# Four gate tiles of the mixer moved ahead of the index logits and ahead of the sparse branch's logits

## The reference, cut to what matters

```python
proj = h @ w_in                                  # fox qkv, dsa qkv, index q/k/w, sb qkv, gates
o_fox = fox_attention(fq, fk, fv, log_f)         # 6 heads: softmax attention with forget terms
o_dsa = dsa_sparse_attention(dq, dk, dv, q_idx, k_idx, w_idx, 64)
                                                 # 5 heads; a score from 8 index heads picks 64 keys per query
o_sb  = stick_breaking_attention(sq, sk, sv)     # 5 heads
g = sigmoid(gates.reshape(b, s, 3, 1024))
merged = g[:, :, 0] * (o_fox @ w_fox_out) + g[:, :, 1] * (o_dsa @ w_dsa_out) + g[:, :, 2] * (o_sb @ w_sb_out)
x = x + merged @ w_out
```

## Time and profile before

| what | value |
|---|---|
| median of 3 executions | 2512.96 us (2512.77 to 2521.8) |
| the profiled execution | 2521.01 us |
| its span, first to last instruction | 2519.2 us |
| mean granted TensorE clock | 0.986 |
| TensorE busy | 2451.9 us (97%) |
| VectorE busy | 827.4 us (33%) |
| ScalarE busy | 248.1 us (10%) |
| DMA | 340.40 MB, 135 GB/s |

### The profile page before, as it was taken

The page is one execution under the profiler, slowest core; times in us unless marked ns, Lnnn a source line. Parts: engine busy times, 40 slices in busy tenths (PEclk is TensorE's granted clock), DMA queues, the critical chain, the costliest instruction groups (busy, mean ns, idle before and its releaser), DMA issues.

```text
span 2519.2 us, 28186 instructions
## 1 busy us (share of the span) xinstructions
PE 2451.9 (97%) x11907; PEld 2111.4 (84%) x11907; DVE 827.4 (33%) x1734; ACT 248.1 (10%) x424; POOL 14.1 (1%) x27
## 2 busy tenths in 40 slices
PE   6999999999999999999999999998999999999998
PEld 5888888878888888888877888887878888878887
DVE  2111323734210111022273331105646512566531
ACT  1000003201100000000311110001210000120000
POOL 0000000000000000000000000000000000000000
PEclk9999999999999999999999999999899999899999
DMA  6544543334554555454523445545335545435542
GB/s 187 155 140 155 130 139 101 101 117 134 140 155 156 150 151 151 150 146 104 153 76 117 134 134 153 155 143 126 110 98 153 143 153 135 110 117 150 156 146 80
DMA packets 491781, 340.40 MB, mean 135 GB/s; under 512 B 47836, under 2 KB 468488, under 8 KB 491656
## 3 DMA queue, kind: packets, MB, share of 16 engines
q1 hardware_dynamic: 487056, 335.53, 46.4%
q10 hardware_dynamic: 4328, 2.02, 0.3%
q0 software_dynamic: 272, 1.05, 0.1%
HBM read 337.52 MB, written 1.05 MB: 134 GB/s over the span
## 4 chain that ended last, share of the span: by engine, by line
PE 82%; issue 10%; DVE 5%; ACTq 1%; DVEq 1%; ACT 0%; DMA 0%; POOLq 0%; POOL 0%
PE bank L494 48%; PE bank L536 21%; PE bank L500 4%; PE bank L768 2%; ACTq L1033 1%; PE bank L894 1%; PE bank L771 1%; DVE work L1245 1%; PE bank L623 1%; PE bank L716 0%; PE bank L714 0%; DVE topw L1569 0%; DVE arena L1248 0%; DVE small L1587 0%; DVEq L1590 0%
## 5 line engine op out<-in xcount | busy, mean ns | idle before, releaser
L494 PE MATMUL bank<-hT,ring 128*128 128x256 f32 (+1 forms) x5952 | 1308.0, 381 | 11.8 <-DVE work L1245 7.7
L494 PEld LDWEIGHTS bank<-hT,ring 128*128 128x128 f32 (+1 forms) x5952 | 1124.2, 189 | 183.3 <-issue 11.2
L536 PE MATMUL bank<-work,ring 128*128 128x256 f32 (+1 forms) x2368 | 515.6, 380 | 0.0
L536 PEld LDWEIGHTS bank<-work,ring 128*128 128x128 f32 (+1 forms) x2368 | 448.4, 190 | 66.4 <-issue 6.1
L1248 DVE SCALAR_TENSOR_TENSOR xT<-bank,xT 128x512 f32<-128x512 f32 x48 | 33.2, 692 | 490.4 <-PE bank L536 490.4
L1245 DVE TENSOR_TENSOR a<-e,bank 128x256 f32<-128x256 f32 x80 | 33.7, 421 | 472.7 <-PE bank L494 472.7
L494 PE MATMUL bank<-xg,ring 128*128 128x256 f32 x640 | 148.9, 390 | 5.7 <-DMA ring<-in_ffn_w_gu 3.6
L494 PEld LDWEIGHTS bank<-xg,ring 128*128 128x128 f32 x640 | 123.1, 195 | 23.4 <-DMA ring<-in_ffn_w_gu 4.0
L1039 ACT ACTIVATE hT<-xT 128x512 f32<-128x512 f32 x56 | 35.4, 632 | 689.3 <-DVE xT L1248 672.9
L536 PE MATMUL bank<-arena,ring 128*128 128x256 f32 x384 | 88.5, 391 | 4.6 <-DVE arena L1248 4.6
L536 PEld LDWEIGHTS bank<-arena,ring 128*128 128x128 f32 x384 | 74.7, 196 | 15.8 <-DVE arena L1248 5.0
(11 more groups left out here) (249 smaller groups left out, 1349.5 us busy)
## 6 DMA issues: line engine op xcount, KB each, us to landing
ring<-in_ffn_w_gu SPq DMA_DIRECT2D x176, 512.0 KB, 5.1
ring<-in_ffn_w_down SPq DMA_DIRECT2D x64, 1024.0 KB, 4.8
ring<-in_ffn_w_up SPq DMA_DIRECT2D x84, 512.0 KB, 5.3
ring<-in_w_in SPq DMA_DIRECT2D x78, 512.0 KB, 5.1
ring<-in_w_in SPq DMA_DIRECT2D x26, 1024.0 KB, 5.2
ring<-in_w_out SPq DMA_DIRECT2D x16, 1024.0 KB, 4.8
ring<-in_ca_w_kv SPq DMA_DIRECT2D x8, 1024.0 KB, 5.1
ring<-in_w_in SPq DMA_DIRECT2D x24, 256.0 KB, 4.0
```

Of the source, the lines that this page charges most:

```text
L494: mm = pe.matmul(b[0:width, 0:S], view[:, c, a:a + width], src[:, c, :], start=(c == 0), stop=(c == C - 1))
L536: return pe.matmul(acc(m), view[0:r, k % 2, m * P:(m + 1) * P], self.src[0:r, self.order[k], :], start=(k == 0 and m % 2 == 0), stop=(k == ...
```

## The change

In `attention1` of TensorE's program, the gate tiles G10 and G11 are computed ahead of the index logits instead of behind them, and G18 and G19 ahead of the sparse logits instead of behind them. No other engine's program changes, the number of instructions is the same, and so is the order in which gate tiles, loads and semaphore counts follow each other among themselves.

```diff
                         mm.then_inc(sem["attn_done"], 1)
+                gate_tiles(2)
                 for t in range(T):
                     w = P * (t + 1)
                     for g in sharing(N_IDX):
...
-                gate_tiles(8)
+                gate_tiles(6)
                 pe.wait_ge(sem["operand_ready"], n("operand_ready"))
                 turn(sc, N_FOX)
...
                     mm.then_inc(sem["attn_done"], 1)
+                gate_tiles(2)
                 for t in range(T):
                     w = P * (t + 1)
                     for g in sharing(N_DSA):
...
-                gate_tiles(6)
+                gate_tiles(4)
                 pe.wait_ge(sem["operand_ready"], n("operand_ready"))
                 turn(sc, N_DSA)
```

## The result

The changed kernel is slower by 0.37%: the ratio to the kernel before is 1.0037 (1.0025 to 1.0049), +9.3 us (+6.3 to +12.3). The median of 12 executions is 2526.19 us against 2513.82 us of 12 before. The medians lie 12.4 us apart, just outside the ratio's interval. The executions of both kernels come in two groups 6 to 7 us apart (before: eight at 2512.5 to 2514.8, four at 2519.0 to 2521.8; after: four at 2520.5 to 2521.6, eight at 2525.8 to 2528.8), and each median lies in the larger group, the lower one before and the upper one after. The forecast was +5.1 us and 2518.1 us; the direction and the mechanism held, the size was too small, and the median lies 0.2 us above the top of the range.

What follows compares the result with a forecast made beforehand. TensorE, busy 97% of the span, was taken as the bound, with VectorE's 39.3 us block setting its second wait. +6.7 us at equal clocks less 1.6 of clock gave +5.1: 2512.96 + 5.1 = 2518.1 us, range 2512 to 2526.

Steps and rivals of the forecast that it cites:

- What bounds the stage: Between forget logits and second transposes: VectorE's fixed 39.3 us block, first index bank to copy of first weighted sum.
- Part 1: G10, G11 ahead of index logits: VectorE starts 6.57 us later; waits of 1.6 us before G12, 1.2 before G16.
- Part 2: G18, G19 ahead of sparse logits: TensorE idle 4.5 us instead of 1.54; shorter work behind it gives back 3.2 us.
- The sum at equal clocks: Both mixers: 6.57 - 3.2 = +3.4 us for a layer, +6.7 us for both, if the sparse softmax stays hidden.
- The clock term: Loss to TensorE's slow clock behind the waits, both layers: 3.8 us after against 5.4 before, -1.6 us.
- (a): Rival: the clock doesn't fall in the changed stretch; +1.3 us, 2514.3 us; chance 0.12.
- (b): Rival: the gate tiles fill both waits, and the clock stays up; -12 us, 2501 us; chance 0.04.
- (c): Rival: clock stays at 0.50 through sparse logits and tiles behind the longer wait; +11.5 us, 2524.5 us; chance 0.10.
- (d): Rival: the sparse softmax ends later than the four tiles, and the transposes wait; +9 us, 2522 us; chance 0.07.
- three signs that I would be wrong: VectorE's copy less than 6 us later, transposes waiting for VectorE, or the clock low for more than 7 us.

Runs made afterwards that it cites:

- the second move: Only G18 and G19 moved ahead of the sparse logits, against the kernel before: 0.9981, 2509.24 us; run once more: 0.9987, 2510.55 us.
- the first move alone: Only G10 and G11 moved ahead of the index logits, against the kernel before: 1.0081, +20.4 us.

## Why the prediction was right in kind and short in size

**What bounds the stage**, a block of 39.3 us on VectorE that starts with the first index bank: right. It kept its length in the changed kernel and in the variants with one and with two tiles in front.

**Part 1**: the shift of +6.57 us was 6.9 us (7.0 less 0.1 for the other overlap at its start). I had taken 0.35 us off because VectorE was busy until 437.20; but its first index read stands 0.75 us behind the first index product in both kernels (437.20 - 436.45 and 442.05 - 441.30), idle before it or not, so nothing was to be taken off. With that the wait ahead of G12 stayed at 1.91 us, not 1.6; the one ahead of G16 was 1.02 us, not 1.2. Its cost of nothing was right: it only shortens the wait ahead of G19, which ends with VectorE's copy.

**Part 2**: 4.17 us against 4.5, ended by the copy in L1488, and no wait ahead of the transposes, with 2.3 us to spare against 2.5 forecast. The work behind the release, 19.5 us by the sum, took 503.39 - 481.85 - 1.9 = 19.6 us.

**The sum at equal clocks** was forecast at +6.7 us. After, it is 139.2 - 1.9 - 3.2 = 134.1 us; before, 128.5 - 1.9 = 126.6 us in the usual execution, its 1.9 us being what 24.6 us are above the 22.7 of the sum. That is +7.5 us. The rest is the larger shift.

**The clock term failed.** I wrote "3.8 against 5.4 in all, -1.6 us". The 3.8 was 5.1 (1.9 and 3.2 us in the two layers; the filled wait gave 4.7 us back). The 5.4 was the worse error: it came from one profiled execution that lay 8 us above the median, and I carried its clock loss over to the median as it stood. In the three later executions it is about 1.9 us, and 0.3 more at most in layer 1 (63.3 us, where the copy at 39.9, 0.5 for the release and the 22.7 give 63.0), since the clock fell for a shorter time in layer 0 and at a harmless place in layer 1. So the term is 5.1 - 1.9 = +3.2 us instead of -1.6, and the sum 7.5 + 3.2 = +10.7 us less 0.2 for the overlap, against the measured +9.3.

The Trainium skill, "TensorE: Matmul & The Clock Gate", section "Why this matters for your kernels", warned of the longer gap, and this trace agrees: 4.17 and 3.52 us of idleness, each with 0.50 right behind. Its price by the section "Terms", half of the slow time, fits too: 3.4 + 6.8 us at 0.50, half of it 5.1 us. The runs show more than that: the clock also fell behind the waits of 1.5 to 1.6 us of layer 0 in all four profiles of the kernel before, and behind the 1.9 us waits of layer 1 in some. What rival (a) counted for itself, that the waits of 1.92 us ahead of G10 lowered nothing, held only in the profile that I had read: the three later ones have 0.50 right behind that wait in layer 1.

**The rivals.** (a), no fall of the clock, did not come; the variant with the wait filled shows its size, +5.8 us rather than +1.3, because the kernel before usually loses little. (b) did not come, for the reason given: the in-order programs let VectorE start later. Its second half alone did come true where the second move stood by itself. (c) did not come for the changed kernel; with the first move alone the slow stretch of layer 1 reached 10.2 us, but TensorE was idle in 3.8 of them and lost 3.1, not 5.1. (d) did not come. Of the three signs that I would be wrong none came, the last one narrowly: the clock stayed low for 6.8 us, not more than 7.

## What to carry to other kernels

Filler work put in front of the products that feed the other engine's long serial block delayed that block by the filler's whole time here (3.5 us for one tile, 7.0 for two); filler behind them, up to the place where the bank is freed, cost nothing and filled the wait. When a wait ends at a bank, look at what stands ahead of the read that frees it: in the changed kernel, moving three copies 6.2 us up gave back the whole slowdown. And before a term of some microseconds is taken from one profile, ask where its execution lies among the others: here 3.5 of the 5.4 us by which the sum was short were that.

## What the runs showed of the hardware that I had not expected

TensorE's granted clock fell without any idle time in front. In the second profile of the kernel with the second move only (2517.01 us, windows of layer 1, columns as before):

```profile
1240.00:1258.00 18.00, 18.00 (x95) 14.32 (x93) 3.80 (x10) 1.53 (x4) 0.00 (x0) 1.00 0.38 117
1258.00:1275.00 17.00, 17.00 (x52) 11.21 (x51) 3.42 (x9) 0.00 (x0) 0.00 (x0) 0.51 0.00 0
```

TensorE is busy by its records throughout, with the forget logits' small products (operands of 64x256, 128x256 and 128x128), and yet the clock stayed at 0.51 for 17 us. The first profile of the same kernel had 1.00 there and took 2509.45 us. The forget logits from 1258.12 on took 15.0 us up to the index logits, where the same work takes 8.2 us in the kernel before (1264.13 to 1272.36), so 6.8 us were lost on them; the two times lie 7.6 us apart. Where the clock falls, and for how long, changed from one execution to the next at the same waits: in the kernel before it was low for 6.8 us once behind the second wait of layer 0 (1.54 us) and for 3.4 us in the three other executions (1.57 us). Such falls are as large as the effect measured here; that they make up all of the spread between executions is likely and wasn't shown.
